# Entry of the two MLPs in a hybrid retention / RG-LRU diffusion step: first group written out, accumulators copied into, norm sums moved into the next unit, last residual update one tile earlier

## The chip, the cores and the metric

The kernel runs on one core of one Trainium2 chip. The metric is the device time of one execution in microseconds (us); lower is better. Three runs of the kernel before gave 2553.63, 2550.53 and 2546.39 us, so the median is 2550.53 us. The profile shown here is of one further execution.

The engines of the core are TensorE (PE, matrix products), VectorE (DVE), ScalarE (ACT), GpSimd (POOL) and SyncE (SP, which here only issues transfers). They run on their own instruction streams and meet through semaphores. PEld is the part of TensorE that loads weights, which overlaps its products.

## What is computed

1024 latent tokens and 128 context tokens pass through a trunk of two layers. The kernel holds all 1152 tokens as columns: `x[:, k, :]` is tile k of the residual, 128 channels by 1152 tokens, with eight tiles for 1024 channels. The latents and the context have modulations of their own, so many operations fall into a piece of 1024 columns and one of 128.

```python
for l in range(DEPTH):                       # two layers
    h = rmsnorm(x, norm_mix[l]) * (1 + sc1) + sh1
    mix = ...                                # l = 0: retention and a gating MLP; l = 1: RG-LRU
    x = x + g1 * mix                         # mix ends in a projection, 1024 x 1024
    h = rmsnorm(x, norm_mlp[l]) * (1 + sc2) + sh2
    ff = square(relu(h @ mlp_w1[l])) @ mlp_w2[l]     # 1024 -> 4096 -> 1024
    x = x + g2 * ff
y = rmsnorm(x, final_norm)
```

The change lies where `x = x + g1 * mix` ends and the two MLPs begin.

## The kernel before

**Precision.** Every matrix product is made of three passes on numbers split into a high and a low part: high by high, low by high, high by low. POOL or ACT makes the high part of a weight unit and POOL the low part (`w_lo`, weight minus high part). ACT makes the high part `h_hi` of an activation tile and DVE the low part `h_lo`. One tile of 128 channels against all tokens is nine matmuls of 384 columns (three passes, three thirds of the tokens); a unit of work is eight tiles.

**End of the mixer, `out_proj` (PE, line 1147; DVE, line 1974).** PE projects eight units. As each comes out, DVE adds it to the residual (`updated`, line 1966), ACT squares the new residual tile (line 1388) and DVE adds the square to `sumsq` (`add_square`, line 1863). The norm's root isn't waited for: the tile times its gain is split at once (`high_direct` on ACT, `low_direct` on DVE, lines 1942 and 1944), and 1/rms multiplies the results of the MLP's first matrix instead. The eight `low_direct` steps stand in one loop. Residual tile 7 is updated between the steps of tiles 5 and 6, and its square is added between those of tiles 6 and 7.

**Norm sums (`norm_waits`, line 957).** The sum over channels is a product of `sumsq` with ones, one matmul (line 970) for each third of the tokens. PE makes the three behind tiles 5, 6 and 7 of the MLP's unit 0. The first waits for all seven additions (`sq_added`); the second and third wait until ACT has read the one before (line 1410, `roots`). DVE then makes three reciprocals (line 1951).

**The MLP, `split_mlp` (PE line 1249, DVE line 2037, ACT line 1496, POOL line 807, SP line 639).** The 4096 hidden channels form eight groups of four units. Units of `mlp_w1` are called unit 0, 1, 2 and so on here. `scale` (lines 2014 and 2017) takes a finished unit out of PSUM times 1/rms; ACT adds the bias, makes the relu and the square; `even` and `odd` form sums of halves (line 2029) and their low parts (line 2034) for a Strassen-like second product. That second product makes 28 products in a group (`second` on PE, line 1287), which DVE adds into accumulators that lie in the place of `x` (`reads`, line 2067; the old residual is in DRAM, `x_spill`). PSUM holds two units, so unit n+2 can start only when `scale` has read unit n; the third product of the first `second` needs `scale` of unit 4.

Seven groups are a hardware loop `Fori(0, SEVEN_GROUPS)` on each engine; unit 0 stands ahead of it, and each turn runs units 1 to 4 and then the 28 products. Ahead of the loop DVE clears all eight tiles of `x` (line 2095), as the first products are added to what lies there:

```python
                scale(None, 0)
                dve.wait_ge(x_spilled, SPILLED[l])
                dve.wait_ge(h_ready, H_NORM[norm - 1] + KT)
                dve.memset(x[:], 0.0).then_inc(cleared, 1)
```

In the first MLP, DVE also sums the modulations of layer 1 between its other steps (`pair_ops`, line 1922, from weights that SP loads by quarters). The second MLP has none of that.

**POOL in the MLP.** `whole_unit` (line 813) casts a unit of weights to its high part (line 820) and subtracts for the low part (line 822), 1024 columns each. For unit 1 it starts when the projection's last unit has freed the weight buffer, so while DVE is in its `low_direct` steps.

**Loads.** SP issues the weight loads in a fixed order, each waiting for the split two units back, with the loads of the modulation quarters between them, which wait for DVE's `pair_ops`.

## Time and profile before

| | |
|---|---|
| runs | 2553.63, 2550.53, 2546.39 us; median 2550.53 us |
| profiled execution | 2553.42 us, of which the span of the trace is 2551.4 us |
| granted TensorE clock, mean | 0.991 of full |
| TensorE matmuls | 2490.0 us busy, 98% of the span |
| VectorE | 1888.5 us, 74% |
| ScalarE | 928.9 us, 36% |
| GpSimd | 902.2 us, 35% |
| DMA | 200.18 MB, mean 78 GB/s |

A busy share says how much of the span the engine had an instruction at work; the rest of its time it waited. Each row of a timeline gives the start in us from the start of the span, the duration in us, the engine, the line in the kernel, the operation, output<-inputs with shapes, and how many instructions were merged into the row. In brackets stands the idle time of the engine just before, and whose instruction ended it. The matrix engine has two clock levels, 1.2 and 2.4 GHz; the column PEclk is the mean granted clock of a stretch as a share of the upper one.

### The profile page before, as it was taken

The numbers are of one execution on the slowest core, as the hardware profiler recorded it, in microseconds if no ns is written. First come the engines' busy times: TensorE is split into PE (matmuls) and PEld (weight loads), VectorE is DVE, ScalarE is ACT, GpSimd is POOL, SyncE is SP. The second block draws the span as 40 slices with busy tenths as digits, with TensorE's granted clock in tenths as the row PEclk, the third lists the DMA queues.
The fourth block names the chain that finished last, engine by engine and source line by source line (L and its number), as shares of the span: only waits on it lengthen the run. The fifth ranks groups of instructions, "written<-read, shape, count | busy, mean of one in ns | idle before, by whom it ended". The sixth has DMA issues, their size and how long they took to land.

```text
span 2551.4 us, 43716 instructions
## 1 busy us (share of the span) xinstructions
PE 2490.0 (98%) x15458; PEld 2434.1 (95%) x15458; DVE 1888.5 (74%) x2918; ACT 928.9 (36%) x1528; POOL 902.2 (35%) x757
## 2 busy tenths in 40 slices
PE   7999999998999999999999999999999999999998
PEld 6999999898999999999999888799999999999998
DVE  6878878779888788888877888946756556656674
ACT  5333322223332332332325666803422432432424
POOL 1221212322545544544532000122445545545540
PEclk9999999999999999999999999999999999999999
DMA  6422322342222222122133111132111111111141
GB/s 248 160 74 71 91 67 81 133 147 76 64 73 86 66 78 79 60 84 85 58 124 111 42 41 41 38 136 88 34 50 49 33 49 49 33 49 49 35 130 75
DMA packets 238666, 200.18 MB, mean 78 GB/s; under 512 B 9461, under 2 KB 229365, under 8 KB 236918
## 3 DMA queue, kind: packets, MB, share of 16 engines
q1 hardware_dynamic: 236580, 179.43, 22.6%
q10 hardware_dynamic: 2002, 19.65, 2.0%
q8 instruction: 51, 0.84, 0.1%
q14 instruction: 33, 0.27, 0.0%
HBM read 174.92 MB, written 24.13 MB: 78 GB/s over the span
## 4 chain that ended last, share of the span: by engine, by line
PE 85%; DVE 10%; issue 2%; ACT 1%; DMA 0%; POOL 0%; SPq 0%; DVEq 0%; ACTq 0%; POOLq 0%
PE psum L921 53%; PE psum L1287 25%; PE psum L1340 2%; DVE mod_sum L1892 2%; PE psum L1195 2%; DVE h_lo L1942 1%; PE psum L1185 1%; DVE sumsq L1951 0%; DVE s_bwd L2331 0%; DVE sumsq L1863 0%; DVE pair_sum L1922 0%; DVE xc L2441 0%; PE psum L1117 0%; DVE b_sum L2029 0%; DVE mod_sum L1887 0%
## 5 line engine op out<-in xcount | busy, mean ns | idle before, releaser
L921 PE MATMUL psum<-h_hi,w_hi 128*128 128x384 f32 (+1 forms) x2880 | 673.5, 342 | 20.9 <-POOL w_lo L785 5.7
L921 PE MATMUL psum<-h_hi,w_lo 128*128 128x384 f32 (+1 forms) x2880 | 661.1, 338 | 0.0
L921 PE MATMUL psum<-h_lo,w_hi 128*128 128x384 f32 (+1 forms) x2880 | 660.5, 337 | 0.0
L921 PEld LDWEIGHTS psum<-h_hi,w_hi 128*128 128x128 f32 x2880 | 514.7, 189 | 36.6 <-issue 21.1
L2067 DVE TENSOR_TENSOR x<-x,psum 128x576 f32<-128x576 f32 x560 | 407.0, 751 | 175.4 <-PE psum L1287 172.8
L921 PEld LDWEIGHTS psum<-h_lo,w_hi 128*128 128x128 f32 x2880 | 519.2, 189 | 0.0
L921 PEld LDWEIGHTS psum<-h_hi,w_lo 128*128 128x128 f32 x2880 | 519.1, 189 | 0.0
L1287 PE MATMUL psum<-b_hi,w_hi 128*128 128x288 f32 x1568 | 337.0, 297 | 2.1 <-DVE even_raw L2017 2.0
L1287 PE MATMUL psum<-b_lo,w_hi 128*128 128x288 f32 x1568 | 336.4, 296 | 0.0
L1287 PE MATMUL psum<-b_hi,w_lo 128*128 128x288 f32 x1568 | 336.3, 296 | 0.0
L848 POOL TENSOR_TENSOR w_lo<-w_sum,w_hi 128x256 fp32r<-128x256 f32 x168 | 155.7, 930 | 322.5 <-ACT w_hi L1581 321.9
L1287 PEld LDWEIGHTS psum<-b_hi,w_hi 128*128 128x128 f32 x1568 | 253.3, 189 | 2.5 <-DVE even_raw L2017 2.2
L1287 PEld LDWEIGHTS psum<-b_lo,w_hi 128*128 128x128 f32 x1568 | 253.3, 189 | 0.0
L1287 PEld LDWEIGHTS psum<-b_hi,w_lo 128*128 128x128 f32 x1568 | 253.3, 189 | 0.0
L820 POOL CAST w_hi<-w_raw 128x1024 fp32r<-128x1024 f32 x70 | 80.5, 1150 | 475.0 <-PE psum L921 294.6
L783 POOL CAST w_hi<-w_raw 128x1024 fp32r<-128x1024 f32 x42 | 45.3, 1079 | 521.5 <-DMA w_raw<-in_ab_w_in 236.2
L1922 DVE SCALAR_TENSOR_TENSOR pair_sum<-pair_raw,cond,pair_sum 128x256 f32<-128x256 f32 x336 | 190.5, 625 | 10.7 <-DMA pair_raw<-in_mod_w 10.0
L1581 ACT ACTIVATE w_hi<-w_sum 128x256 fp32r<-128x256 f32 x168 | 80.6, 488 | 299.2 <-PE psum L1287 166.2
L822 POOL TENSOR_TENSOR w_lo<-w_raw,w_hi 128x1024 fp32r<-128x1024 f32 x70 | 176.3, 2519 | 5.6
L1892 DVE SCALAR_TENSOR_TENSOR mod_sum<-mod_raw,cond,mod_sum 128x128 f32<-128x128 f32 x448 | 147.0, 398 | 4.0 <-DMA mod_raw<-in_mod_w 1.7
L2034 DVE TENSOR_TENSOR b_lo<-b_sum,b_hi 128x576 fp32r<-128x576 f32 (+1 forms) x140 | 144.5, 1080 | 3.0
L848 POOL TENSOR_TENSOR w_lo<-w_raw,w_hi 128x512 fp32r<-128x512 f32 x112 | 138.1, 1252 | 1.3 <-ACT w_hi L1581 1.0
(327 smaller groups left out, 3017.3 us busy)
## 6 DMA issues: line engine op xcount, KB each, us to landing
w_raw<-in_mlp_w SPq DMA_DIRECT2D x128, 512.0 KB, 3.9
pair_raw<-in_mod_w SPq DMA_DIRECT2D x96, 256.0 KB, 2.8
mod_raw<-in_mod_w SPq DMA_DIRECT2D x64, 256.0 KB, 2.9
w_raw<-in_ab_w_in SPq DMA_DIRECT2D x24, 512.0 KB, 4.7
x_spill<-x ACTq DMA_DIRECT2D x2, 4608.0 KB, 14.7
x_old<-x_spill SPq DMA_DIRECT2D x16, 576.0 KB, 5.7
w_raw<-in_lru_w_in SPq DMA_DIRECT2D x16, 512.0 KB, 4.1
x_spill<-x ACTq DMA_DIRECT2D x4, 1728.0 KB, 6.8
```

What stands on the lines that cost most here:

```text
L820: pool.tensor_copy(hi[:, s, :], w_raw[:, s, :]).then_inc(hi_done, 1)
L822: pool.tensor_tensor(lo[:, s, :], w_raw[:, s, :], hi[:, s, :].bitcast(F32), ALU.subtract).then_inc(split_done, 1)
L848: pool.tensor_tensor(lo, of, hi.bitcast(F32), ALU.subtract).then_inc(signal, inc)
L921: mm = pe.matmul(psum[:, s, c, 0:end - c * CH], w, v[:, k, c * CH:end], start=(first and n == 0 and w is hi[k] and v is in_hi), stop=(last ...
L1195: mm = pe.matmul(y_bank(i), w[n], v[:, n, bank_tokens(c)], start=(first and n == 0 and m == 0), stop=(last and n == GRP - 1 and m == 2))
L1287: mm = pe.matmul(banks[:, pair + b, 0:HB], w, v[:, p, hb, b * HB:(b + 1) * HB], start=(p == 0 and m == 0), stop=(p == 1 and m == 2))
L1340: last_mm = pe.matmul(psum[:, s, c, 0:CH], gate_w[:, 2 * d + kind, :], xc[:, c * CH:(c + 1) * CH], start=True, stop=True)
L1581: act.activation(dst, src, ACT.Copy).then_inc(w_part_hi, 1)
L1892: op = dve.scalar_tensor_tensor(out=total, in0=w, scalar=s, in1=total, op0=ALU.mult, op1=ALU.add)
L1922: dve.scalar_tensor_tensor(out=total, in0=w, scalar=s, in1=total, op0=ALU.mult, op1=ALU.add).then_inc(pair_step, 1)
L2034: dve.tensor_tensor(lo, src, hi.bitcast(F32), ALU.subtract).then_inc(block_ready, 1)
L2067: last = dve.tensor_tensor(t, t, banks[:, pair:pair + 2, 0:HB], op)
```

## The change

- **DVE, `out_proj`**: the update of residual tile 7 stands ahead of the `low_direct` step of tile 5 (`UPDATE_BEHIND` = 5) and no longer behind it, and the last `add_square` behind the step of tile 7 and no longer ahead of it.
- **ACT, `out_proj`**: the high part of tile 7 is made ahead of its square.
- **POOL, `firsts`**: the subtraction for unit 1's low weights waits until five `low_direct` steps are done (`quiet`).
- **PE**: the sums of squares are made behind tile 7 of unit 0 and behind tiles 0 and 1 of unit 1.
- **DVE, PE**: group 0 is written out ahead of the loop, which runs from 1. POOL, ACT and SP keep their loops from 0.
- **DVE, `reads`**: the memset and its semaphore are gone. In group 0 the first product that goes to an accumulator block is copied into it, or multiplied by -1 where it would have been subtracted (`FIRST_ADDS`). Of the 40 writes of accumulators in a group 16 become such copies.

```diff
+UPDATE_BEHIND = KT - 3
+FIRST_ADDS = ((0, Y22), (0, Y12), (1, Y11), (3, Y21))
...
                     pool.wait_ge(hi_done, at(g, GRP_UNITS, c + 1))
+                    for signal, value in quiet:
+                        pool.wait_ge(signal, value)
                     pool.tensor_tensor(lo[:, s, :], w_raw[:, s, :], hi[:, s, :].bitcast(F32), ALU.subtract).then_inc(split_done, 1)
...
-                    whole_unit(g, U + 1, ((product_done, at(g, PER_GROUP, DONE0 + past(l, PER_GROUP) - 3)), (unit_done, U)))
+                    whole_unit(g, U + 1, ((product_done, at(g, PER_GROUP, DONE0 + past(l, PER_GROUP) - 3)), (unit_done, U)),
+                               quiet=((h_ready, H_NORM[2 * l + 1] + UPDATE_BEHIND),))
...
+            def sum_of_squares(n, c):
+
+                if BANKS * n + c:
+                    pe.wait_ge(ssq_read, BANKS * n + c)
+                pe.matmul(ssq_psum[:, 0:CH], ones[:], sumsq[:, c * CH:(c + 1) * CH], start=True, stop=True).then_inc(ssq_done, 1)
+
+            def late_norm_waits(n):
+                def before(k):
+                    pe.wait_ge(h_ready, H_NORM[n] + k + 1)
+
+                def behind(k):
+                    if k == KT - 1:
+                        pe.wait_ge(sq_added, (KT - 1) * (n + 1))
+                        sum_of_squares(n, 0)
...
                     def behind(k):
+                        if first_head(g) and k < BANKS - 1:
+                            sum_of_squares(2 * l + 1, k + 1)
...
-                first(None, 0, *norm_waits(2 * l + 1))
-                with pe.Fori(0, SEVEN_GROUPS) as g:
+                first(None, 0, *late_norm_waits(2 * l + 1))
+
+                def group(g):
                     firsts(g, False)
                     for u in range(GRP):
                         second(g, u, U + GRP + 1 + u)
+
+                group(0)
+                with pe.Fori(1, SEVEN_GROUPS) as g:
+                    group(g)
...
                     else:
                         item_out(act, None, 0, AT_OUT[l].items + KT - 1)
-                        square_tile(norm, KT - 1)
                     high_direct(norm, k)
+                square_tile(norm, KT - 1)
...
                 for k in range(KT):
+                    if k == UPDATE_BEHIND:
+                        updated(KT - 1)
                     low_direct(norm, k)
-                    if k == KT - 3:
-                        updated(KT - 1)
-                    if k == KT - 2:
-                        add_square(norm, KT - 1)
+                add_square(norm, KT - 1)
...
-                            t = block(u, dst).rearrange("p (b t) -> p b t", b=2)
-                            last = dve.tensor_tensor(t, t, banks[:, pair:pair + 2, 0:HB], op)
+                            t, product = block(u, dst).rearrange("p (b t) -> p b t", b=2), banks[:, pair:pair + 2, 0:HB]
+                            if not first_head(g) or (j, dst) not in FIRST_ADDS:
+                                last = dve.tensor_tensor(t, t, product, op)
+                            elif op == ALU.add:
+                                last = dve.tensor_copy(t, product)
+                            else:
+                                last = dve.tensor_scalar(t, product, -1.0, None, ALU.mult)
...
-                dve.memset(x[:], 0.0).then_inc(cleared, 1)
-                dve.wait_ge(cleared, SPLIT_MLP.index(l) + 1)
-                with dve.Fori(0, SEVEN_GROUPS) as g:
+
+                def group(g):
...
+                group(0)
+                with dve.Fori(1, SEVEN_GROUPS) as g:
+                    group(g)
```

**VectorE, end of the first layer's `out_proj`, from the low part of tile 4 (its first row) to the first reciprocal.** `h_lo` is the low part of a tile, `x<-psum,mod,x` the residual update, `sumsq` the sum of squares. Before:

```order
L1942 SCALAR_TENSOR_TENSOR h_lo<-x,gain,h_hi 128x1024 [waits part_hi]
...
L1942 SCALAR_TENSOR_TENSOR h_lo<-x,gain,h_hi 128x1024 [waits part_hi]
...
L1966 SCALAR_TENSOR_TENSOR x<-psum,mod,x 128x768 [waits unit_done]
...
L1942 SCALAR_TENSOR_TENSOR h_lo<-x,gain,h_hi 128x1024 [waits part_hi]
...
L1863 TENSOR_TENSOR sumsq<-sumsq,square_out 128x1152 [waits sq_added,sq_ready]
L1942 SCALAR_TENSOR_TENSOR h_lo<-x,gain,h_hi 128x1024 [waits part_hi]
...
L1951 RECIPROCAL sumsq<-sumsq 128x384 [waits ssq_read] x3
```

Changed:

```order
L1973 SCALAR_TENSOR_TENSOR h_lo<-x,gain,h_hi 128x1024 [waits part_hi]
...
L1997 SCALAR_TENSOR_TENSOR x<-psum,mod,x 128x768 [waits unit_done]
...
L1973 SCALAR_TENSOR_TENSOR h_lo<-x,gain,h_hi 128x1024 [waits part_hi]
...
L1973 SCALAR_TENSOR_TENSOR h_lo<-x,gain,h_hi 128x1024 [waits part_hi]
...
L1973 SCALAR_TENSOR_TENSOR h_lo<-x,gain,h_hi 128x1024 [waits part_hi]
...
L1894 TENSOR_TENSOR sumsq<-sumsq,square_out 128x1152 [waits sq_added,sq_ready]
L1982 RECIPROCAL sumsq<-sumsq 128x384 [waits ssq_read] x3
```

The update has moved up by one tile and the addition of the last square down by one.

**TensorE, end of unit 0 and start of unit 1 of the first MLP.** `psum<-sumsq,ones` is a sum of squares over channels; the first rows are tile 7 of unit 0. Before:

```order
L970 MATMUL psum<-sumsq,ones 128x384 [waits ssq_read]
L921 MATMUL psum<-h_hi,w_hi 128x384 [waits h_ready]
...
L921 MATMUL psum<-h_hi,w_lo 128x386
L970 MATMUL psum<-sumsq,ones 128x384 [waits ssq_read]
L1297 UNCONDITIONAL_BRANCH
L1297 ISA
L908 ISA [waits pair_read]
L938 ISA [waits read_out_1]
L921 MATMUL psum<-h_hi,w_hi 128x384 [waits split_done]
```

Changed:

```order
L928 MATMUL psum<-h_hi,w_hi 128x384 [waits h_ready]
...
L928 MATMUL psum<-h_hi,w_lo 128x386
L983 MATMUL psum<-sumsq,ones 128x384 [waits ssq_read,sq_added]
L928 MATMUL psum<-h_hi,w_hi 128x384 [waits split_done,read_out_1,pair_read]
...
L928 MATMUL psum<-h_hi,w_lo 128x386
L983 MATMUL psum<-sumsq,ones 128x384 [waits ssq_read]
L928 MATMUL psum<-h_hi,w_hi 128x384 x2
```

Of the three sums one is left at the end of unit 0, with the wait for the last square; the other two have gone into unit 1, and no branch lies between the units.

**VectorE, from the scaling of unit 0 to the first sums of group 0.** Before:

```order
L2014 COPY bias<-psum 128x2 [waits unit_done,rstd_ready]
L2017 TENSOR_TENSOR even_raw<-psum,sumsq 128x384 x3
L2095 MEMSET x 128x9216 [waits h_ready,x_spilled]
L2097 UNCONDITIONAL_BRANCH [waits cleared]
L2097 ISA
L2040 ISA [waits squared]
L2029 TENSOR_TENSOR b_sum<-even_raw 128x576 [waits product_done]
```

Changed:

```order
L2044 COPY bias<-psum 128x2 [waits unit_done,rstd_ready]
L2047 TENSOR_TENSOR even_raw<-psum,sumsq 128x384 x3
L2059 TENSOR_TENSOR b_sum<-even_raw 128x576 [waits squared,product_done,h_ready,x_spilled]
L2064 TENSOR_TENSOR b_lo<-even_raw,b_hi 128x576 [waits block_hi]
```

The first sum now follows the scaling directly and takes over the memset's waits beside its own wait for ScalarE's squares.

## Rows read from the trace of the kernel before

**Rows 1.** Timeline of TensorE: every row behind an idle gap that the argument names.

```profile
577.84 0.79 PE L921 MATMUL psum<-h_hi,w_hi 128*128 128x384 f32 x3 [1.36 <-DVE h_lo L1944]
585.27 1.02 PE L970 MATMUL psum<-sumsq,ones 128*128 128x384 f32 x2 [2.45 <-DVE sumsq L1863]
...
619.20 0.79 PE L921 MATMUL psum<-h_hi,w_hi 128*128 128x384 f32 x3 [0.93 <-DVE b_sum L2017]
...
635.72 0.79 PE L921 MATMUL psum<-h_hi,w_hi 128*128 128x384 f32 x3 [2.89 <-DVE even_raw L2017]
...
656.50 0.53 PE L1287 MATMUL psum<-b_hi,w_hi 128*128 128x288 f32 x2 [2.00 <-DVE even_raw L2017]
...
1769.31 0.91 PE L970 MATMUL psum<-sumsq,ones 128*128 128x384 f32 x2 [2.35 <-DVE sumsq L1863]
...
2488.05 0.45 PE L1195 MATMUL psum<-hid_hi,w_hi 128*128 128x384 f32 x1 [1.77 <-DVE hid_lo L2090]
```

**Rows 2.** Windows of TensorE: stretch, length, busy (instructions), PEclk, DMA share, GB/s.

```profile
560.00:660.00 100.00, 90.31 (x500) 0.95 0.26 79
585.00:590.00 5.00, 4.73 (x15) 0.66 0.21 88
656.00:662.00 6.00, 5.50 (x30) 0.72 0.38 128
2488.00:2493.00 5.00, 4.96 (x28) 1.00 0.00 0
```

**Rows 3.** Timeline of VectorE, end of the first layer's `out_proj`.

```profile
574.03 3.69 DVE L1942 SCALAR_TENSOR_TENSOR h_lo<-x,gain,h_hi 128x1024 fp32r<-128x1024 f32 x2
...
580.76 1.67 DVE L1966 SCALAR_TENSOR_TENSOR x<-psum,mod,x 128x768 f32<-128x768 f32 x3
582.34 1.54 DVE L1942 SCALAR_TENSOR_TENSOR h_lo<-x,gain,h_hi 128x1024 fp32r<-128x1024 f32 x2
...
583.87 1.35 DVE L1863 TENSOR_TENSOR sumsq<-sumsq,square_out 128x1152 f32<-128x1152 f32 x1
...
590.63 4.96 DVE L1951 RECIPROCAL sumsq<-sumsq 128x384 f32<-128x384 f32 x2 [1.10 <-ACT sumsq L1410]
```

**Rows 4.** Timeline of GpSimd in the same stretch.

```profile
573.96 2.41 POOL L822 TENSOR_TENSOR w_lo<-w_raw,w_hi 128x1024 fp32r<-128x1024 f32 x1
```

**Rows 5.** Timeline of VectorE, first MLP: scaling of unit 0, memset, first sum.

```profile
595.71 1.48 DVE L2017 TENSOR_TENSOR even_raw<-psum,sumsq 128x384 f32<-128x384 f32 x3
599.05 7.74 DVE L2095 MEMSET x<- 128x9216 f32 x1 [1.87 <-issue]
607.10 2.88 DVE L2029 TENSOR_TENSOR b_sum<-even_raw 128x576 f32<-128x576 f32 x1 [0.32 <-DVE x L2095]
```

**Rows 6.** Timeline of ScalarE: the squares of unit 0.

```profile
598.42 0.93 ACT L1525 ACTIVATE even_raw<-even_raw 128x384 f32<-128x384 f32 x2
```

**Rows 7.** Timeline of VectorE, first MLP: scaling of unit 2 and of unit 4.

```profile
634.11 1.47 DVE L2017 TENSOR_TENSOR even_raw<-psum,sumsq 128x384 f32<-128x384 f32 x3
...
654.97 1.48 DVE L2017 TENSOR_TENSOR even_raw<-psum,sumsq 128x384 f32<-128x384 f32 x3
```

**Rows 8.** Timeline of TensorE: unit 1 of the first MLP begins.

```profile
591.75 0.98 PE L921 MATMUL psum<-h_hi,w_hi 128*128 128x384 f32 x3
```

**Rows 9.** Timeline of TensorE, second MLP: tiles 4 and 5 of unit 0, first of unit 1.

```profile
1763.66 0.69 PE L921 MATMUL psum<-h_hi,w_hi 128*128 128x384 f32 x3
...
1765.23 0.68 PE L921 MATMUL psum<-h_hi,w_hi 128*128 128x384 f32 x3
...
1775.80 0.98 PE L921 MATMUL psum<-h_hi,w_hi 128*128 128x384 f32 x3
```

**Rows 10.** Timeline of VectorE: low part of tile 4 ahead of the second MLP.

```profile
1759.59 3.43 DVE L1942 SCALAR_TENSOR_TENSOR h_lo<-x,gain,h_hi 128x1024 fp32r<-128x1024 f32 x1
```

**Rows 11.** Groups of VectorE by line: count, busy us, mean ns, idle before and releaser.

```profile
L2067 DVE TENSOR_TENSOR x<-x,psum 128x576 f32<-128x576 f32 x560 | 407.0, 751 | 175.4 <-PE psum L1287 172.8
```

**Rows 12.** DMA queues between 560 and 700 us: packets, MB, share of 16 engines.

```profile
q8 instruction: 7, 0.11, 0.3%
```

8 lines of the change are left out of this document (3 added, 5 removed).

## The prediction

> **What bounds the kernel now.** I read the busy shares first: TensorE has matmuls for 98% of the span, so almost all of the time is its work, and an edit can give back only what it idles or runs slowly. Next I read TensorE's timeline for idle gaps. Around the first MLP's entry there are five [rows 1]: 1.36, 2.45, 0.93, 2.89 and 2.00 us, 9.63 in all, and the window 560 to 660 shows 100 - 90.31 = 9.69 us idle [rows 2], so nothing else is missing there. Each is ended by VectorE. From 656.50 us to the end of that MLP there is no gap. At the second entry there is one, 2.35 us [rows 1]. Third, the windows: behind the gap of 2.45 us the granted clock is 0.66 over 5 us, behind that of 2.00 it is 0.72 over 6 us [rows 2], so part of each runs at 1.2 GHz and about 5 x 0.34 = 1.7 us of work is lost; a gap of 1.77 us is followed by 1.00 [rows 1, 2]. Last, VectorE and GpSimd around the entries, for what made VectorE late.
>
> **Unit 0, first MLP.** A tile takes TensorE 1765.23 - 1763.66 = 1.57 us [rows 9]. A low part takes VectorE 1.53 us, the distance of rows 582.34 and 583.87; but tile 3's took 3.69, as GpSimd's subtraction (573.96, 2.41 us) was at work [rows 3, 4]: 573.96 + 2.41 + 1.53 = 577.90, near its end at 577.72. So VectorE waits out GpSimd's instruction. The hold takes that away: tiles 3 and 4 end at 574.03 + 2 x 1.53 = 577.1. GpSimd subtracts from 577.15 to 579.55, beside the update (1.6 us), which ends at 578.7.
>
> What the update costs beside a subtraction no row shows at that spot; the bounds are 0 and the full 2.4. I take 0, by the nearest operation that also has one input in PSUM and one in SBUF: the accumulations average 751 ns over 560 [rows 11] though GpSimd subtracts beside many of them. The Trainium skill (SBUF — State Buffer, section "Who interferes with whom") says that the shared port pair is an exclusive lock, that a VectorE instruction with at most one SBUF input doesn't contend, and that one with two waits for a GpSimd instruction that reads SBUF. By it the update costs 0 and tile 5 is held; the trace agrees on the second (3.69 against 1.54) and bears out the first by the 751 ns alone.
>
> Tile 5 is held to 579.55 and ends at 581.1, tile 6 at 582.6, tile 7 at 584.15, the last addition (1.35) at 585.5. TensorE is free at 577.84 - 1.36 = 576.5 and makes tiles 3 and 4 until 579.6, waits 1.5 us for tile 5, and ends tile 7 at 581.15 + 3 x 1.57 = 585.9, when the sum is ready. Its matmul counts as two instructions of 384 columns, of which nine take 1.57: 0.35 us. Unit 1 begins at 586.2, not 591.75 [rows 8], with two sums (0.7) still ahead in it: 4.85 us earlier. The gap of 1.5 us lies between 1.36 and 1.77, neither followed by a slow stretch.
>
> **Group 0, first MLP: VectorE decides.** From the first sum's matmul to the first reciprocal passes about 1.7 us as now (585.27; the reciprocals end at 595.59 [rows 1, 3]). Three reciprocals of 4.96 / 2 us back to back from 587.5 end at 595.0: 0.6 earlier. Scaling of unit 0 ends at 596.6 instead of 595.71 + 1.48 = 597.19.
>
> Between that end and the first sum at 607.10 lie 9.91 us, the memset with its 1.87 ahead and 0.32 behind (I count the 1.87 as part of it) [rows 5]. What is late next is ScalarE: its squares end at 598.42 + 0.93 = 599.35, 2.16 us behind the scaling [rows 5, 6]. So the memset gives 9.91 - 2.16 = 7.75, with the 0.6 above 8.35.
>
> Everything VectorE does from there to the scaling of unit 4 is as before, and TensorE had long finished the units it reads: the scaling of unit 2 ends at 635.58 - 8.35 = 627.2, of unit 4 at 656.45 - 8.35 = 648.1 [rows 7]. TensorE against that: units 1 and 2 took 591.75 to 618.27 (619.20 less its gap), 26.5, now 586.2 + 0.7 + 26.5 = 613.4; unit 3 took 13.6 (to 635.72 - 2.89), now to 627.0, so the gaps of 0.93 and 2.89 shrink to about 0 and 0.2. From there to the last gap it took 18.8, of it some 1.5 at the slow clock behind the 2.89: 17.3, to 644.6. It then waits 3.6 us for the scaling of unit 4 and goes on at 648.2 instead of 656.50: **8.3 us**. Of TensorE's gain one part is thus handed back in a longer last gap. The slow stretch behind it stays.
>
> GpSimd's subtractions collide with VectorE here too: the first sum took 2.88 for 576 columns [rows 5]. The change shifts who meets whom. Bounds: one collision of 2.4 us more, or up to all of the final wait gone (3.6 us, and the 1.7 slow behind it). I take 0, as GpSimd's work is the same and VectorE is nearly always busy.
>
> **Second MLP.** No modulation sums, so TensorE never waits for VectorE behind 1775.80; the memset there lies beside TensorE's units and its removal is worth 0. If that cover were thinner it would cost up to 9.6. Tile 4's low part was held (3.43 us for its first piece [rows 10]); now it ends at 1761.1, the update at 1762.7, tile 5, held by the subtraction, at 1765.1, tiles 6 and 7 at 1766.6 and 1768.1, the addition at 1769.4. TensorE wants them at 1765.23, 1766.8 and 1768.4 and the sum at 1769.95: no gap, and none of the slow stretch. Unit 1 begins at 1770.3, not 1775.80 [rows 9], less 0.7: **4.8 us**. Bounds: 0 (a gap like today's returns) and 4.8.
>
> **Edits together at nothing.** 16 accumulator writes of 40 in a group become copies: at most 751 ns as now, off the path. ScalarE's order (high part before square): its square, 1.2 us, is done before the low part of tile 7 is. The hold of `w_lo` for unit 1: ready at 579.6, wanted at 586.2; SP's next load waits for it and lands long before GpSimd's next cast. Written-out groups: see below.
>
> **Sum.** 8.3 + 4.8 = 13.1 us, 2553.42 to 2540.3 for the profiled execution; that stood 2.9 above the median of 2550.53, so I say **2537.4**.
>
> **Rivals.**
> 1. *More collisions*: with the memset gone VectorE's two-input operations meet GpSimd's subtractions where it stood still or cleared, and the stretch to unit 4 loses 2.4 to 4 us. For: the first sum's 2.88. Against: the same subtractions are in today's stretch. Gain 9 to 10.5: 2541. 0.18.
> 2. *Fewer collisions*: VectorE's chain shortens until TensorE's work ends last: 3.6 + 1.7 more, 18.4 in all: 2532. Against: GpSimd's times follow TensorE, not VectorE's idle moments. 0.10.
> 3. *The hold backfires*: tiles 5 to 7 come later than worked out, at both entries a gap above 2 us returns with its slow stretch. The second entry then gives nothing; the first keeps what VectorE's chain gives, less about 2: gain 6, 2544.5. 0.10.
> 4. *Slower*: the written-out groups stall on instruction fetch. Between 560 and 700 us 7 instruction packets land on one queue [rows 12], in code run once or for the first time. If a written-out group added as many and each stopped TensorE, 14 packets for two groups would have to cost (13.1 + 7.65) / 14 = 1.5 us each to make it slower; at 2 us it is 2565. Against: all idle of the window 560 to 660 but 0.06 us has a named cause, with most of those packets in or near it. The Trainium skill (Runtime: NRT & Kernel Launch, "Instruction fetch mechanics") says that sequential code is fetched ahead and that a taken branch out of the window stalls; by it this rival has no price. No run here shows a branch's. 0.04.
> 5. *It doesn't do what it says*: VectorE still starts group 0 late, since the first sum inherits the waits for the spill of `x`. The memset had them too and started at once but for its 1.87, which then would be a wait. Gain 11.5, inside the range; counted with the forecast.
>
> Forecast as worked out: 0.58.
>
> **How the numbers follow.** Bounds 18.4 and about 6 us give 2532 to 2544.5; half a microsecond of scatter of a median on either side: **2531.5 to 2545**. Within 0.3% (7.65 us, about what can be told from no change) fall rival 3 and a corner of rival 1: same 0.14. Slower 0.04. Faster 0.82.
>
> **What would show it.** Right: TensorE goes from unit 0 to 1 at the second entry without a gap and at clock 1.00; at the first a gap of about 1.5 us ahead of tile 5, almost none ahead of units 3 and 4, and one of 3 to 4 us ahead of the third product of group 0, ended by the scaling of unit 4. VectorE's first sum starts 2.2 us behind the scaling of unit 0. Wrong: a last gap above 5 us (rival 1), none (rival 2), a gap ahead of the first sum of squares (rival 3), idle TensorE in group 0 that no semaphore ends (rival 4).

## The result and the profile after

The kernel after takes 2534.72 us, median of four runs (2533.68 to 2535.75); the kernel before took 2550.61 us beside it (four runs, 2546.39 to 2553.63). The ratio is 0.9942, with a 95% interval of 0.993 to 0.9954: 0.6% faster. Predicted were 2537.4 us, with a range of 2531.5 to 2545.

| | before | after |
|---|---|---|
| profiled execution | 2553.42 us | 2534.76 us |
| span of the trace | 2551.4 us | 2532.3 us |
| granted TensorE clock, mean | 0.991 | 0.995 |
| VectorE busy | 1888.5 us | 1865.8 us |
| rest from the end of tile 2 of unit 0, first MLP | 1974.9 us | 1960.4 us |

The last row needs a word. The two traces already stand 4.5 us apart at 50 us, where the programs are the same, so the spans say too much about the change. The rest is counted from the moment at which TensorE has finished tile 2 of unit 0 of the first MLP: nothing of the change acts on TensorE before it. (Expectations that speak of "tile 5 to the end" count from the start of tile 5 instead, which is 3.14 us and the gap ahead of tile 5 later; there the four traces of after have 1956.2, 1955.7, 1957.7 and 1957.8 us.) In the trace before, that is the start of the gap ahead of tile 3, 577.84 - 1.36 = 576.48 [rows 1]; in the one after, tiles 3 and 4 (2 x 1.57 us) lie between it and the gap ahead of tile 5, so 576.08 - 1.01 - 3.14 = 571.93.

**The first entry after.** TensorE's timeline; each row is start, duration, engine, line, operation, and in brackets the idle time ahead and what ended it. These are all its gaps there, against the five of [rows 1], and the start of unit 1 against [rows 8]:

```profile
576.08 0.79 PE L928 MATMUL psum<-h_hi,w_hi 128*128 128x384 f32 x3 [1.01 <-DVE h_lo L1975]
...
581.27 0.98 PE L928 MATMUL psum<-h_hi,w_hi 128*128 128x384 f32 x3
...
638.46 0.53 PE L1313 MATMUL psum<-b_hi,w_hi 128*128 128x288 f32 x2 [1.65 <-DVE b_lo L2064]
...
643.11 0.50 PE L1313 MATMUL psum<-b_hi,w_hi 128*128 128x288 f32 x2 [2.00 <-DVE even_raw L2047]
```

Of 9.63 us of gaps 1.01 + 1.65 + 2.00 = 4.66 are left. To compare places, 5.11 us are added to the time after: VectorE's low part that stood at 571.71 in the trace before starts at 566.60 here. Unit 1 then begins at 581.27 + 5.11 = 586.38, and was at 591.75.

VectorE in the same stretch, against [rows 3, 5, 7]. `even_raw` is a scaled unit, `b_sum` a sum of halves, `b_hi` and `b_lo` the high and low part of such a sum:

```profile
571.97 1.66 DVE L1997 SCALAR_TENSOR_TENSOR x<-psum,mod,x 128x768 f32<-128x768 f32 x3
573.55 2.41 DVE L1973 SCALAR_TENSOR_TENSOR h_lo<-x,gain,h_hi 128x1024 fp32r<-128x1024 f32 x2
...
582.38 7.38 DVE L1982 RECIPROCAL sumsq<-sumsq 128x384 f32<-128x384 f32 x3 [2.03 <-ACT sumsq L1441]
...
589.87 1.48 DVE L2047 TENSOR_TENSOR even_raw<-psum,sumsq 128x384 f32<-128x384 f32 x3
593.72 0.76 DVE L2059 TENSOR_TENSOR b_sum<-even_raw 128x576 f32<-128x576 f32 x1 [2.37 <-ACT even_raw L1556]
...
609.45 7.38 DVE L2064 TENSOR_TENSOR b_lo<-b_sum,b_hi 128x1152 fp32r<-128x1152 f32 x4
...
634.88 6.49 DVE L2064 TENSOR_TENSOR b_lo<-b_sum,b_hi 128x1152 fp32r<-128x1152 f32 x4
...
641.49 1.48 DVE L2047 TENSOR_TENSOR even_raw<-psum,sumsq 128x384 f32<-128x384 f32 x3
```

and GpSimd, whose subtraction is now held until the low part of tile 4 is done:

```profile
572.20 2.41 POOL L828 TENSOR_TENSOR w_lo<-w_raw,w_hi 128x1024 fp32r<-128x1024 f32 x1 [3.43 <-DVE h_lo L1975]
```

The update (three pieces, 1.66 us) runs beside the subtraction and isn't slowed; tile 5's low part (2.41 against 1.54) is. The first sum starts 2.37 us behind the scaling of unit 0 and waits for ScalarE: in the trace before, 9.91 us lay between them. The gap of 1.65 us lies inside the first product, where TensorE needs a low part that VectorE hasn't made yet; the gap of 2.00 us is the one ahead of the third product. Scaling of unit 4 starts at 641.49 + 5.11 = 646.60 instead of 654.97, 8.37 us earlier.

**The second entry after.** No gap is left; the three sums now stand at 1755.04, 1757.24 and 1759.46, the last two inside unit 1:

```profile
1755.04 0.81 PE L983 MATMUL psum<-sumsq,ones 128*128 128x384 f32 x2
1755.39 0.98 PE L928 MATMUL psum<-h_hi,w_hi 128*128 128x384 f32 x3
...
1757.24 0.81 PE L983 MATMUL psum<-sumsq,ones 128*128 128x384 f32 x2
```

**The clock.** Windows of TensorE as in [rows 2]: stretch, length, busy (instructions) of each engine, granted clock, share of DMA, GB/s.

```profile
560.00:660.00 100.00, 95.34 (x583) 93.78 (x582) 91.15 (x138) 44.08 (x87) 40.61 (x34) 1.00 0.26 81
643.00:649.00 6.00, 5.89 (x44) 5.92 (x45) 5.69 (x9) 3.80 (x10) 4.20 (x6) 1.00 0.32 114
1755.00:1765.00 10.00, 10.00 (x55) 9.20 (x54) 8.47 (x7) 2.18 (x4) 3.42 (x2) 1.00 0.19 52
```

Behind the gap of 2.00 us the clock is 1.00 here. In the trace before it was 0.72 behind a gap of the same length, and the section on both kernels again shows it at 0.72 or 0.73 in the three other traces of after.

### The profile page after: what moved, and what is told of

The parts are those of the page before. It is cut to its first block, busy times and chain, and to the rows that moved or that the text cites. A ratio compares the mean times of both kernels' runs of the same rounds, so it can differ in the third digit from the quotient of the medians.

```text
span 2532.3 us, 43499 instructions
## 1 busy us (share of the span) xinstructions
PE 2480.3 (98%) x15458; PEld 2426.6 (96%) x15458; DVE 1865.8 (74%) x2916; ACT 927.2 (37%) x1528; POOL 909.8 (36%) x757
## 4 chain that ended last, share of the span: by engine, by line
PE 86%; DVE 9%; issue 2%; ACT 1%; DMA 0%; POOL 0%; SPq 0%; DVEq 0%; ACTq 0%; POOLq 0%
PE psum L928 55%; PE psum L1313 25%; PE psum L1371 2%; DVE mod_sum L1923 2%; PE psum L1219 2%; PE psum L1209 1%; DVE sumsq L1982 1%; DVE pair_sum L1953 1%; DVE b_lo L2064 0%; DVE h_lo L1973 0%; DVE s_bwd L2369 0%; DVE xc L2479 0%; PE psum L1141 0%; PE psum L1131 0%; DVE mod_sum L1918 0%
## 5 line engine op out<-in xcount | busy, mean ns | idle before, releaser
L2098 DVE TENSOR_TENSOR x<-x,psum 128x576 f32<-128x576 f32 x528 | 383.6, 751 | 166.5 <-PE psum L1313 163.9
```

Of the source, the lines that this page charges most:

```text
L2098: last = dve.tensor_tensor(t, t, product, op)
```

## The experiments

Since the start of the program varies between executions by several microseconds, each is read by its median and, for the mechanism, by the rest defined above. The runs together:

| kernel | median us (runs) | ratio to before, 95% | tile 2 ends at | rest | start of scaling of unit 4, from tile 2's end |
|---|---|---|---|---|---|
| before, first profile | 2550.61 (4) | | 576.48 | 1974.9 | 78.5 |
| before again | 2549.73 (1) | | 575.21 | 1972.5 | 76.3 |
| after, first profile | 2534.72 (4) | 0.993 to 0.9954 | 571.93 | 1960.4 | 69.6 |
| after again, 1 | 2532.04 (1) | | 569.93 | 1959.9 | 69.6 |
| after again, 2 | 2539.78 (9) | 0.9941 to 0.9973 | 575.07 | 1962.4 | 70.1 |
| after again, 3 | 2535.35 (6) | 0.9943 to 0.9972 | 570.41 | 1962.0 | 69.7 |
| memset back | 2540.36 (10) | 0.9952 to 0.9983 | 570.49 | 1965.2 | 74.8 |
| norm order back | 2543.98 (10) | 0.9965 to 0.9995 | 575.52 | 1965.9 | 70.6 |
| no hold | 2537.25 (10) | 0.9938 to 0.9965 | 570.00 | 1963.0 | 71.1 |
| written out only | 2548.97 (10) | 0.998 to 1.0009 | 571.65 | 1972.8 | 78.0 |
| pair steps later | 2537.55 (8) | 0.9933 to 0.9968 | 576.25 | 1961.9 | 69.5 |
| sums in unit 0 | 2542.43 (10) | 0.9963 to 0.9992 | 570.88 | 1968.5 | 71.9 |
| early splits | 2540.43 (5) | 0.9953 to 0.9979 | 575.93 | 1962.4 | 70.0 |
| scaling between | 2533.45 (5) | 0.9932 to 0.9959 | 572.59 | 1959.0 | 66.9 |

Rest is the span less the time at which tile 2 ends. "No hold" has its first gap ahead of tile 3, at 571.12 - 1.12.

The rows were not all timed side by side, nor on one chip. The kernel before, timed beside them, had a median of 2550.61 us for the first profiles, 2547.78 (19 runs) for before again, after again 1, memset back and norm order back, 2550.35 (28) for after again 2, no hold, written out only and pair steps later, 2550.48 (17) for after again 3, sums in unit 0 and early splits, and 2548.32 (9) for scaling between. So a median is compared either by its ratio, or with the kernel after that was timed beside it.

### Both kernels again

No edit.

> The kernel before, once more, for a second trace of it. In the first pair of traces the kernel before is 4.55 us later already at its first tiles (48 us from the start), far ahead of the change. Theory A (the start varies by chance from execution to execution, with the loads): this trace differs from the first one by 1 to 6 us at 48 us, and then runs parallel to it within 0.5 us to the first MLP. Theory B (the longer program changes the start): it is within 0.5 us of the first one at 48 us too. By both, the two entries cost the same as in the first trace: from the update of tile 7 on, TensorE idles 9.6 us at the first and 2.35 us at the second.

> The changed kernel, once more, for a second trace. Theory A: its start, too, moves by some us against its first trace. Theory B: within 0.5 us of it. Both: gaps of 1.0, 1.65 and 2.0 us at the first entry, none at the second. Whether the stretch behind the 2.0 us gap (at about 643 us) runs at clock 1.00 again, or at about 0.72 as in the kernel before, tells whether the missing slow stretch belongs to the change (the gap is now cut in two by two products) or is chance.

> The kernel after once more, timed beside the three others of this call so that they are compared on one chip. Expected: 2534.7 (the four runs of the result spread from 2533.7 to 2535.8), ratio to the kernel before 0.994. If the median of the result was partly chance of the start-up, it lies up to 2538 here, since the sum of the two entries alone (8.3 and 4.1 us in the traces) takes only 12.4 us off the 2550.5 of before.

> The kernel after once more, on the same chip as the two before it. Expected 2534 to 2539, and 1956 to 1958 us from tile 5 of the first entry to the end of the span, whatever the start-up takes.

Before again: 2549.73 us, rest 1972.5. After again: 2532.04, 2539.78 and 2535.35, rests 1959.9, 1962.4, 1962.0. Tile 2 ends anywhere from 569.9 to 575.1 us with one and the same program. With the programs that have the old norm order it ends from 571.7 to 576.5, with the variants of after at up to 576.3 (pair steps later), so both kinds reach both ends. One source is TensorE's clock early in the execution. The same window in the traces before, after, and after again 2:

```profile
36.00:42.00 6.00, 5.99 (x26) 5.67 (x26) 2.19 (x6) 3.95 (x6) 0.00 (x0) 0.68 0.95 339
```

```profile
36.00:42.00 6.00, 5.75 (x35) 5.44 (x36) 4.11 (x9) 5.74 (x9) 0.00 (x0) 1.00 0.93 331
```

```profile
36.00:42.00 6.00, 5.76 (x27) 5.44 (x26) 1.90 (x5) 3.93 (x7) 0.00 (x0) 0.70 0.93 329
```

The clock is 0.68 and 0.70 in two of them and 1.00 in one, of two different programs. It isn't the only source: in the trace of before again this window has 1.00 as well, and tile 2 ends at 575.2. So far as these traces show, what the start takes is chance and not the change. The mean rest is 1973.7 us for the two traces of before and 1961.2 for the four of after: **12.5 us** belong to the change. All 20 runs of the kernel after have a median of 2535.8 us (2532.0 to 2543.3), all 77 of the kernel before 2550.3 (2544.0 to 2561.3): 14.5 us, of which the start can hold the other two.

The trace of before again also has both gaps with another clock behind them:

```profile
583.38 0.91 PE L970 MATMUL psum<-sumsq,ones 128*128 128x384 f32 x2 [2.43 <-DVE sumsq L1863]
...
653.04 0.53 PE L1287 MATMUL psum<-b_hi,w_hi 128*128 128x288 f32 x2 [1.99 <-DVE even_raw L2017]
```

```profile
583.00:588.00 5.00, 4.62 (x23) 4.09 (x24) 4.78 (x6) 2.60 (x5) 0.00 (x0) 1.00 0.21 88
652.00:658.00 6.00, 4.96 (x26) 4.96 (x27) 4.48 (x8) 3.99 (x9) 4.02 (x5) 0.72 0.42 132
```

Behind 2.43 us the clock is 1.00 here; it was 0.66 behind 2.45 us in the first trace [rows 1, 2]. Behind 1.99 us it is 0.72. A gap of that length may be followed by a slow stretch or not.

The expectation for after again 1 asked whether the missing slow stretch behind the last gap belongs to the change. It doesn't. The same window behind the last gap (1.99, 1.99 and 2.01 us) in after again 1, 2 and 3:

```profile
641.00:647.00 6.00, 5.90 (x33) 5.93 (x34) 4.38 (x7) 3.36 (x9) 3.59 (x5) 0.72 0.33 114
647.00:653.00 6.00, 6.00 (x35) 6.00 (x35) 4.37 (x7) 3.16 (x8) 3.62 (x5) 0.72 0.27 94
642.00:648.00 6.00, 6.00 (x36) 6.00 (x36) 4.39 (x7) 3.06 (x8) 3.54 (x5) 0.73 0.26 91
```

The slow stretch is there in three of the four traces of after; only the first profile lacks it. From the end of tile 2 to the third product these four take 71.2, 71.2, 71.7 and 71.3 us, the two of before 80.0 and 77.8: 7.6 us between the means.

### The memset back

```diff
                 dve.wait_ge(h_ready, H_NORM[norm - 1] + KT)
+                dve.memset(x[:], 0.0).then_inc(cleared, 1)
+                dve.wait_ge(cleared, SPLIT_MLP.index(l) + 1)
...
-                            if not first_head(g) or (j, dst) not in FIRST_ADDS:
+                            if True:
```

> The changed kernel with VectorE's memset of x put back ahead of group 0, and group 0's products all added. Theory 1 (VectorE's chain from the scaling of unit 0 to that of unit 4 decides at the first entry, nothing at the second): 7.5 us slower than the changed kernel (9.6 less the 2.2 us that ScalarE's squares take anyway), up to 9 if a gap above 2 us brings the slow clock back; all of it at the first entry, 0 at the second. Rival (the norm part carries the gain and the memset lay beside other work): under 2 us slower. Time about 2542 to 2544 against 2534.7; by the rival 2536.

2540.36 us and a rest of 1965.2, which is 4.0 us more than the mean of after; the medians differ by 4.6 (from 2535.8), and by the ratios, 0.9967 against 0.9942 to 0.9957, by 2.5 to 6.4. VectorE's timeline shows why it is not 7.5:

```profile
591.80 7.74 DVE L2131 MEMSET x<- 128x9216 f32 x1 [1.87 <-issue]
599.57 0.76 DVE L2060 TENSOR_TENSOR b_sum<-even_raw 128x576 f32<-128x576 f32 x1
...
611.62 3.75 DVE L2060 TENSOR_TENSOR b_sum<-b_sum,even_raw 128x576 f32<-128x576 f32 x2
...
616.20 5.00 DVE L2065 TENSOR_TENSOR b_lo<-b_sum,b_hi 128x1152 fp32r<-128x1152 f32 x4
...
645.31 1.48 DVE L2048 TENSOR_TENSOR even_raw<-psum,sumsq 128x384 f32<-128x384 f32 x3
```

The first sum starts 599.57 - 588.45 = 11.12 us behind the scaling of unit 0, with 3.85 (593.72 - 589.87) in the kernel after: 7.3 us, near the 7.5 expected. But from the first sum to the scaling of unit 4 VectorE takes 645.31 - 599.57 = 45.74 us here and 641.49 - 593.72 = 47.77 in the kernel after, and at the scaling of unit 4 only 74.8 - 69.7 = 5.1 us are left of the 7.3. The collisions fall otherwise: the four low parts take 5.00 us instead of 7.38, two sums ahead of them 3.75 instead of 1.55, and one subtraction of GpSimd lies beside the memset, where in the kernel after (597.88) it lies beside VectorE's `pair_sum` steps:

```profile
596.35 2.40 POOL L829 TENSOR_TENSOR w_lo<-w_raw,w_hi 128x1024 fp32r<-128x1024 f32 x1
```

The memset shifts VectorE against GpSimd, and part of its cost is paid by collisions that it avoids. TensorE's third product, 76.5 us after tile 2, is also 5.1 later than in the kernel after. That the rest is up by 4.0 only goes with the clock: the last gap is 1.42 us here and is followed by 1.00 (window 647 to 653 us), where three of the four traces of after have a slow stretch. The rival that nothing is lost is out; theory 1 has the mechanism and too high a price.

### The order of the norm back

```diff
-                first(None, 0, *late_norm_waits(2 * l + 1))
+                first(None, 0, *norm_waits(2 * l + 1))
...
-                    if k == UPDATE_BEHIND:
-                        updated(KT - 1)
                     low_direct(norm, k)
-                add_square(norm, KT - 1)
+                    if k == KT - 3:
+                        updated(KT - 1)
+                    if k == KT - 2:
+                        add_square(norm, KT - 1)
```

The hold of `w_lo`, the sums in unit 1 and ScalarE's order are undone too; copies and written-out groups stay.

> The changed kernel with the old order of the norm: update of tile 7 behind the low part of tile 5, its square added ahead of tile 7, the three sums of squares in unit 0, no hold of the subtraction. Copies and written-out groups stay. Theory 1: at the first entry only the 0.6 us by which the scaling of unit 0 comes later is lost, since VectorE's chain decides there; at the second the gap of 2.35 us and the slow stretch come back, 4.1 us. Together 4.7 us slower than the changed kernel, about 2539.5. Rival (TensorE's earlier start of unit 1 carries over at both): 4.1 + 4.3 = 8.4 us slower, 2543.

The rest is 1965.9 us, 4.7 more than after: what theory 1 said. VectorE reaches the scaling of unit 4 only 0.9 us later, and TensorE's gap ahead of it shrinks from 3.65 in two pieces to 1.84, so the first entry loses little, although the gap ahead of the sums is back there too (2.43 us, with a clock of 1.00 behind it); at the second entry the gap costs 4.1 us again:

```profile
1759.23 0.91 PE L983 MATMUL psum<-sumsq,ones 128*128 128x384 f32 x2 [2.33 <-DVE sumsq L1892]
```

The median of ten runs, 2543.98, lies 8.2 us above 2535.8, and by the ratios (0.998 against 0.9942 to 0.9957) 5.9 to 9.7, which alone would speak for the rival. Its mechanism isn't in the trace: TensorE's third product comes 72.2 us after tile 2, only 0.9 later than in after. Of the span's 8.4 us above the mean of the four traces of after 3.7 lie in the start (tile 2 ends at 575.5, theirs at 571.8) and 4.7 in the rest. Why the median of ten is as high as this one execution stays open.

### The sums of squares back in unit 0, all else as after

```diff
-                        if first_head(g) and k < BANKS - 1:
-                            sum_of_squares(2 * l + 1, k + 1)
...
-                first(None, 0, *late_norm_waits(2 * l + 1))
+                first(None, 0, *norm_waits(2 * l + 1))
```

> The kernel after with the three column sums of squares back inside unit 0, behind its tiles 5, 6 and 7 (as in the kernel before), while the update ahead, the order on ScalarE and the hold of w_lo stay. The traces of the kernel before have a TensorE gap of 2.43 us ahead of these sums in the first entry and 2.33 us in the second. Theory 1 (it is the place of the sums that makes these gaps, since they wait for VectorE's last addition of squares, which here comes behind the low part of tile 7): a gap on sumsq of 2.4 to 4 us in both entries, now ahead of tile 6's part; unit 1 starts 2.5 to 4 us later in both; in the first entry VectorE's reciprocals start no earlier than in the kernel after, so up to 3 us is lost there, and 3 to 4.5 us in the second entry; from tile 5 of the first entry to the end 1962 to 1964 us, where the kernels after took 1956 to 1958; median 2540 to 2544. Rival (the update ahead alone had removed the wait): no gap on sumsq over 1 us, 1956 to 1958 us from tile 5 to the end, 2536.

2542.43 us, 7.1 above the kernel after timed beside it (2535.35); rest 1968.5, 7.3 above after. From tile 5 to the end it is 1964.4 us, at the upper end of what theory 1 expected. Both entries have the gap:

```profile
579.38 0.91 PE L983 MATMUL psum<-sumsq,ones 128*128 128x384 f32 x2 [2.48 <-DVE sumsq L1892]
...
1757.35 0.91 PE L983 MATMUL psum<-sumsq,ones 128*128 128x384 f32 x2 [2.48 <-DVE sumsq L1892]
```

```profile
580.00:585.00 5.00, 5.00 (x18) 4.26 (x18) 2.87 (x2) 1.16 (x2) 0.00 (x0) 0.66 0.00 0
1758.00:1763.00 5.00, 5.00 (x19) 4.46 (x18) 2.83 (x2) 1.16 (x2) 0.00 (x0) 0.66 0.00 0
```

2.48 us each, with the clock at 0.66 for five microseconds behind. It is the place of the sums that makes the gap: they wait for VectorE's last addition, and TensorE has no work ahead of them that doesn't. The third product comes 73.5 us after tile 2, 2.2 later than in after, and the second entry costs 4.3 us more. What the update moved ahead gives by itself this run doesn't say: the last addition stands behind tile 7's low part here, later than in the kernel before, and sums in unit 0 with the addition at its old place weren't run.

### Without the hold of `w_lo`

```diff
-                               quiet=((h_ready, H_NORM[2 * l + 1] + UPDATE_BEHIND),))
+                               )
```

> The kernel after without the wait that holds GpSimd's first subtraction (w_lo) until VectorE has done the sixth low part. Theory 1 (the subtraction shares VectorE's port and would hold the last update or a low part for its length, 2.41 us): the update of the last tile (1.66 us in the trace of after) or the tile beside it takes some 1 to 2.4 us more, TensorE's gap before a tile of unit 0 grows from 1.0 to between 2 and 3 us in the first entry, and one appears in the second; 2536 to 2538. Rival (the hold only moves the collision to another tile, since in the trace of after tile 5 still takes 2.41 us beside the same subtraction): the gaps keep their sum and the time stays within 1 us of the kernel after, or gets 0.5 us better because w_lo is ready earlier.

```profile
567.24 2.40 POOL L828 TENSOR_TENSOR w_lo<-w_raw,w_hi 128x1024 fp32r<-128x1024 f32 x1
567.30 3.69 DVE L1973 SCALAR_TENSOR_TENSOR h_lo<-x,gain,h_hi 128x1024 fp32r<-128x1024 f32 x2
571.12 0.80 PE L928 MATMUL psum<-h_hi,w_hi 128*128 128x384 f32 x3 [1.12 <-DVE h_lo L1975]
...
575.75 0.79 PE L928 MATMUL psum<-h_hi,w_hi 128*128 128x384 f32 x3 [1.22 <-DVE h_lo L1975]
...
638.09 0.73 PE L1313 MATMUL psum<-b_hi,w_hi 128*128 128x288 f32 x2 [1.63 <-DVE b_lo L2064]
...
642.72 0.50 PE L1313 MATMUL psum<-b_hi,w_hi 128*128 128x288 f32 x2 [0.44 <-DVE even_raw L2047]
...
1750.94 0.79 PE L928 MATMUL psum<-h_hi,w_hi 128*128 128x384 f32 x3 [1.09 <-DVE h_lo L1975]
```

The subtraction starts right behind its cast and holds tile 3's low part (3.69 us), as before the change [rows 3]. (The hold waits for the fifth low part, not the sixth as the expectation says.) At the first entry TensorE has gaps of 1.12 and 1.22 us in place of 1.01, and gets 1.56 back in the last one: 1.12 + 1.22 + 1.63 + 0.44 = 4.41 us in all, against 4.66, so there the gaps keep their sum, as the rival says. The third product still comes 72.7 us after tile 2, 1.4 later than in after, but a slow stretch has moved ahead of it: the clock is 0.66 from 638 to 643 us and 1.00 behind the last gap. At the second entry a gap of 1.09 us stands in place of none, as theory 1 says. That 1.1 us is what the hold is shown to be worth. The rest is 1.8 us above after, inside the 2.5 us by which the rests of one kernel differ, and the median, 2537.25, is 2.5 below the kernel after timed beside it (2539.78), so neither can tell more.

### The groups written out, nothing else

```diff
-                with dve.Fori(0, SEVEN_GROUPS) as g:
+                def group(g):
...
+                group(0)
+                with dve.Fori(1, SEVEN_GROUPS) as g:
+                    group(g)
```

and the same on TensorE, on the kernel before.

> The kernel before with the first group of both MLPs written out on TensorE and VectorE, and nothing else: memset, adds, order of the norm and column sums as before. It measures what the longer program costs by itself. Theory (more instruction packets, no idle TensorE): 2550.5, no difference to before within 1.5 us; the two entries keep their gaps of 2.4 to 3 us; ten more packets on the instruction queue. Rival (instructions come late where code is not in a loop): TensorE shows idle time that no engine releases inside the first group, and the time is 2 to 15 us above before. A gain is expected by neither.

2548.97 us, ratio 0.998 to 1.0009, rest 1972.8 between the two of before. The queue of instruction packets has ten more, here on the page of before and of this kernel:

```profile
q8 instruction: 51, 0.84, 0.1%
```

```profile
q8 instruction: 61, 1.00, 0.2%
```

TensorE's gaps in the first entry all end with a named release of VectorE (1.35, 2.45, 0.32, 3.02 and 1.36 us, 8.50 in all), and its window leaves nothing else, 140 - 131.51 = 8.49:

```profile
560.00:700.00 140.00, 131.51 (x810) 129.22 (x810) 125.05 (x176) 48.20 (x95) 59.02 (x49) 0.96 0.24 73
```

Writing the groups out costs nothing that these runs can tell. The Trainium skill (Runtime: NRT & Kernel Launch, "Instruction fetch mechanics") says that code in sequence is fetched ahead; the trace agrees, with no idle time of TensorE that is not named.

### Two gaps left, and what sets them

Three edits of the kernel after, aimed at the gaps of 1.65 and 2.00 us. First, four `pair_sum` steps taken off VectorE's chain:

```diff
-                    pairs(32, 36)
+                    if not first_head(g):
+                        pairs(32, 36)
...
+                        if l == 0 and first_head(g):
+                            reads(g, u, 32 + 4 * u)
```

> The kernel after, with four of VectorE's pair_sum steps of the first MLP's first group (steps 32 to 35, 1.67 us together in the row at 626.62) taken out of the stretch before the third product, and four steps each put between the reads of its four units. It tests whether the 3.65 us of gaps left before the third product (1.65 for b_lo, 2.00 for the scaling of unit 4) are VectorE's chain of work and nothing else. Theory: the row of b_lo at 634.88 and the scaling at 641.49 start 1.5 us earlier, the two gaps shrink from 3.65 to about 2.1 us, 2533.0. Rival (the chain there is set by ScalarE's b_sum, on which VectorE waited 0.88 us, or GpSimd's splits collide elsewhere): the gaps keep their sum within 0.5 us and the wait for ScalarE grows instead; 2534.5. Worse is possible only if the later steps delay the weights that pair_sum makes, which would show as a wait of TensorE on pair_sum parts; 2536.

```profile
636.27 1.55 DVE L2059 TENSOR_TENSOR b_sum<-b_sum,even_raw 128x576 f32<-128x576 f32 x2 [2.19 <-ACT b_sum L1556]
...
642.77 0.52 PE L1313 MATMUL psum<-b_hi,w_hi 128*128 128x288 f32 x2 [1.61 <-DVE b_lo L2064]
...
647.42 0.50 PE L1313 MATMUL psum<-b_hi,w_hi 128*128 128x288 f32 x2 [2.01 <-DVE even_raw L2047]
```

The wait for ScalarE grows from 0.88 to 2.19 us and takes the place of the steps: gaps of 1.61 and 2.01 us, rest 1961.9. The rival is right. A new gap of 0.81 us at 691.56, ended by VectorE's additions, comes on top. Second, in addition, ScalarE's three `w_hi` copies ahead of its squares of unit 3, so that GpSimd's subtractions come earlier:

```diff
+                    w_high(g, 0, c, range(3))
                     squares(g, 3)
-                    odd(g, 3, lambda: w_high(g, 0, c, range(3)))
+                    odd(g, 3)
```

> The kernel after with the four pair_sum steps moved as in the experiment before, and ScalarE's three w_hi copies for the third product (0.40 and 0.92 us) put ahead of its squares of unit 3 and not behind them, so that GpSimd's subtractions w_lo (0.74 and 3.59 us beside b_lo) run in the 2.19 us in which VectorE waits for ScalarE. Theory (b_lo takes 6.49 us for four only because GpSimd's w_lo hold VectorE's port: alone, four take 2.9 us by the 0.75 us rows of b_lo): b_lo shrinks to 3.5 to 5 us, the two gaps before the products shrink from 3.6 to between 1 and 2.5 us in the first MLP; 1.5 to 2.5 us less from tile 5 to the end, 1954 to 1956 us. Rival 1 (ScalarE's squares start later by the copies, 1.3 us, and the whole chain with them): the gaps stay within 0.5 us of 3.6. Rival 2 (in the loops the earlier copies make ScalarE wait for the unit before its squares, and TensorE gets gaps in each group): 2 us or more slower, with rows of TensorE that wait in the groups.

```profile
631.79 2.35 POOL L855 TENSOR_TENSOR w_lo<-w_raw,w_hi 128x512 fp32r<-128x512 f32 x2
631.15 3.67 DVE L1954 SCALAR_TENSOR_TENSOR pair_sum<-pair_raw,cond,pair_sum 128x256 f32<-128x256 f32 x4
...
640.85 5.00 DVE L2065 TENSOR_TENSOR b_lo<-b_sum,b_hi 128x1152 fp32r<-128x1152 f32 x4
```

The low parts take 5.00 us and not 6.48, but four `pair_sum` steps, which now meet the subtractions, take 3.67 instead of 1.67, and the scaling of unit 3 behind them starts 58.9 us after tile 2 instead of 56.3. Gaps of 1.60 and 2.00 us, rest 1962.4: no gain (the median, 2540.43, is 5.1 above the kernel after timed beside it, with tile 2 ending at 575.9 in the trace). The gaps stay as rival 1 says, though not for its reason: VectorE waits 2.20 us for ScalarE, as long as without the early copies (2.19). The collision has only changed its victim. Third, VectorE's order alone:

```diff
+                    if p:
+                        low(g, p, 4, H_T3, 1, b_sum[:, p, H_T3, :])
+                        low(g, p, 3, H_O1, 2, odd_raw(p))
+                        blocks_done(g, 10)
+                        scale(g, 4)
```

TensorE waits for the blocks in that order, and `scale(g, 4)` no longer follows all four low parts.

> The kernel after with VectorE's order before the third product changed: the b_lo block that TensorE waits for first (H_T3) ahead of the two that it reads next, and the scaling of unit 4 ahead of the last two b_lo blocks and not behind them. No operation is added or left out. Theory (each of the two gaps left, 1.64 and 2.0 us, ends with one VectorE operation that stands behind others which TensorE needs later): the gap before the first product's second half falls from 1.6 to under 0.5 us, the one before the third product from 2.0 to between 0.5 and 2 us, 1.5 to 3 us less from tile 5 of the first entry to the end: 1953.5 to 1956 us where the kernels after took 1956.2, 1955.7, 1957.7 and 1957.8; nothing changes in the loops. Rival 1 (GpSimd's w_lo hold VectorE's port for as long in any order, so that the scaling is as late as before): the two gaps keep their sum within 0.5 us. Rival 2 (ScalarE's b_hi of H_T3 comes late, since three w_hi copies stand ahead of it there): the first gap stays at 1.3 to 1.6 us and the second shrinks.

```profile
635.91 3.48 DVE L2064 TENSOR_TENSOR b_lo<-b_sum,b_hi 128x576 fp32r<-128x576 f32 x2
...
639.50 1.48 DVE L2047 TENSOR_TENSOR even_raw<-psum,sumsq 128x384 f32<-128x384 f32 x3
...
641.12 0.49 PE L1313 MATMUL psum<-b_hi,w_hi 128*128 128x288 f32 x2 [0.61 <-DVE even_raw L2047]
```

The first gap is gone, the second is 0.61 us; a new one of 1.04 us appears later, at a wait for VectorE's additions. The third product comes 68.5 us after tile 2, 2.8 earlier than in after. The clock is 1.00 behind both (windows 641 to 647 and 650 to 656 us). The rest is 1959.0 us, 2.2 below the mean of after and the shortest of all traces, and from tile 5 to the end it is 1954.5, as the theory expected. That is one trace, and the rests of one kernel differ by 2.5 us. The times can't tell the two apart (ratio 0.9946 against 0.9942 to 0.9957 for after); what the trace shows is 1.65 us of gaps in place of 3.65.

## Why the prediction was right

The forecast, 13.1 us for the two entries, stands against 12.5 us in the mean rests; the time 2537.4 against 2534.72. In the two traces first shown the rests differ by 14.5 us: 8.8 up to the third product, 1.5 behind it, where the clock is 1.00 in the one and 0.72 in the other, and 4.1 at the second entry.

- **First entry, 8.3 us: right.** Counted with the 5.11 us from VectorE's low part, TensorE's third product starts at 643.11 + 5.11 = 648.22 (forecast 648.2), 8.28 us earlier than 656.50. Counted from the end of tile 2 it is 80.0 - 71.2 = 8.8 us in this pair, and 7.6 between the means of all traces. Unit 1 begins at 586.38 (586.2), the scaling of unit 4 ends at 641.49 + 1.48 + 5.11 = 648.08 (648.1). The wait for ScalarE behind the scaling of unit 0 was forecast at 2.16 and is 2.37 us.
- **The gaps.** Ahead of tile 5: 1.5 forecast, 1.01 measured, and 1.01, 1.57 and 1.10 in the three repeats. Ahead of unit 3 none, as forecast. The last one was forecast at 3.6 us in one piece; it comes as 1.65 us for the low parts and 2.00 for the scaling, 3.65 together. That TensorE waits for the low parts inside the first product, before it waits for the scaling, was overlooked, which changed nothing in the sum.
- **Collisions taken at 0: right as a sum.** The first sum's 2.88 us became 0.76, and in exchange four low parts went from 3.36 to 7.38 us. Beside that `pair_sum` steps that took 4.60 us for four now take 1.67. From the first sum to the scaling of unit 4 VectorE takes 654.97 - 607.10 = 47.87 us before and 47.77 after. It is luck as much as judgement: with the memset back, the same work took 45.74.
- **Update beside the subtraction at 0: right**, 1.66 us against 1.67 without. The trace agrees with the lock that the Trainium skill describes (SBUF — State Buffer, "Who interferes with whom"): an operation with one input in PSUM isn't held, the low part with both in SBUF is, 2.41 against 1.54 us.
- **"The slow stretch behind it stays": not in the first trace, but in the three repeats.** The clock behind the last gap is 1.00 in the window 643 to 649 us of the first, which saved 1.5 us more, and 0.72, 0.72 and 0.73 in the others. A gap of 2.0 us was taken to be always followed by what had followed it once; in most traces it is, but not in all. The same holds for the gap ahead of the sums: the second trace of before has 1.00 behind 2.43 us.
- **Two sums inside unit 1 at 0.35 each: too small.** A tile with a sum ahead takes 1757.24 - 1755.04 = 2.20 us, without one 1.57: 0.63 each, the row behind the sum being 0.98 us and not 0.69. The second entry gave 4.1 us and not 4.8; its unit 1 begins at 1755.39 + 15.00 = 1770.39 (forecast 1770.3; 15.00 is the distance of the two traces at tile 4, 1763.66 - 1748.66).
- **Rivals 1 and 2** named a last gap above 5 us, or none; it is 3.65 in two pieces.
- **Rival 3** (the hold backfires) is excluded by the traces of after, with no gap ahead of the first sum of squares, and by the run without the hold, which adds a gap at the second entry. **Rival 4** (instruction fetch) is excluded by the run with the groups only written out. **Rival 5** is too: what ends last ahead of the first sum is ScalarE.
- **What the sum didn't hold**: the executions' start. Tile 2 ends within 5.1 us in the four traces of after and within 1.3 in the two of before, and on average 4.0 us earlier in those of after; that can hold what the medians differ beyond the 12.5 us, but isn't shown to.

## What to carry to other kernels

Where one engine's chain decides, take the operation out that nobody reads soon, and then look for the chain's next late member: here ScalarE 2.4 us behind, then GpSimd's subtractions beside VectorE's low parts. Moving either engine's work mostly moved the collision to another instruction (early splits); beside the memset, which took its usual 7.74 us, a subtraction held nobody up. Changing the order in which results are delivered to the engine that waits took 2.0 us of gaps away in one trace, moving the work none. Compare two traces from a common event close ahead of the change, or the scatter of the start is taken for its effect.

## What the hardware showed that was not expected

- The clock behind a gap isn't fixed by the gap: 0.66 behind 2.45 us and 1.00 behind 2.43 us with the kernel before at the same place; behind the last gap of the kernel after 1.00 once (2.00 us) and 0.72, 0.72 and 0.73 in three further executions (1.99, 1.99 and 2.01 us).
- A memset of 9216 elements has a record of 7.74 us with 1.87 us ahead in which VectorE waits for nothing named. Both belong to its price: without the memset the first sum comes 7.3 us earlier, though a wait for ScalarE of 2.37 us takes its place; 7.3 + 2.37 is about 7.74 + 1.87.
- Whether the effects add up stays open: by the rests, one trace each, memset back costs 4.0 us, the norm's order back 4.7, and both together (the groups written out only) 11.6, with rests of one kernel up to 2.5 us apart. By the medians, against 2535.8, it is 4.6, 8.2 and 13.2, where 12.8 for the two stands against 13.2 for both.
